# Memory heads as three passes over high and low halves, with the queries split straight from PSUM

## The chip, the cores and the metric

The kernel runs on one core of a Trainium2 chip. The metric is the device time of one execution in microseconds (us), the lower the better. A second figure, the span, is the time between the first and the last instruction that the profiler saw on the core. The engines are named as the profile names them: PE (TensorE, matmuls and transposes), PEld (its weight loads), DVE (VectorE), ACT (ScalarE), POOL (GpSimd) and SP (the queue that issues DMAs).

## The reference, cut to what matters

The program is a stack of several blocks in 32-bit floats over 512 tokens of width 1024. The change touches only the memory heads of its first two layers. Each layer normalises the tokens, projects them, runs twelve main heads (a forgetting attention in layer 0, a retention in layer 1) and four memory heads against 256 memory rows, gates all sixteen heads and projects out.

```python
def mem_cross_attention(q_mem, mem_n, w_kv):
    B, S, _ = q_mem.shape                                   # S = 512
    kv = mem_n @ w_kv
    km, vm = split_cols(kv, [MEM_W, MEM_W])
    q = q_mem.reshape(B, S, N_MEM_HEADS, HEAD_DIM)          # 4 heads of 128
    km = km.reshape(B, -1, N_MEM_HEADS, HEAD_DIM)           # 256 memory rows
    vm = vm.reshape(B, -1, N_MEM_HEADS, HEAD_DIM)
    s = jnp.einsum('bshd,bmhd->bhsm', q, km).astype(jnp.float32) / math.sqrt(HEAD_DIM)
    p = jax.nn.softmax(s, axis=-1).astype(vm.dtype)
    return jnp.einsum('bhsm,bmhd->bshd', p, vm).reshape(B, S, MEM_W)
```

In first_block each layer does `h = rmsnorm(x, norm_g[i])`, `proj = h @ w_in`, the main heads, `memo = mem_cross_attention(q_mem, mem_n, w_mem_kv[i])`, `o = concatenate([main, memo]) * silu(z)` and `x = x + o @ w_out[i]`.

## The kernel before, in words

Every large matmul is done in three passes over halves. A 32-bit operand is split into a high half (a copy to the type fp32r) and a low half (the value less the high half, again fp32r), and PE forms high x high, high x low and low x high. Weights arrive as tiles of 128x1024 in a ring of five raw buffers. For each tile ACT writes the high half (`wh`, `copy` at L2208), and DVE (tiles 0 to 72, L1264) or POOL (nearly all later ones, L2855) writes the low half (`wl`) by a subtraction. Both halves stand in rings of three, so the tile of number u + 2 is split while PE is at tile u.

The order of work on each engine is written out by hand, one function per engine: `tensor`, `vector`, `scalar`, `gpsimd`, `sync`. An object `Feed` walks the same plan on each of them. `feed.take()` moves on by one weight tile and puts the split of the tile two ahead into the engine's queue at that place. Between some of these tiles the plan has tiles of another matrix ("ada"), which DVE multiplies by a column and adds up (L1272, L1233). In layer 0 all of them cost DVE two instructions each. A wait on a semaphore holds the whole queue of its engine.

The rmsnorm of the tokens is put off. PE multiplies the tokens unscaled, and the scale of each token (`R` for layer 0, `RS` for layer 1, as a column `rcol`) is applied when a projection leaves PSUM. The queries of two memory heads come from one unit of PE, `unit_f(("qm", i))`. `store_q` on DVE multiplies them by the scale and by -1/sqrt(128) into `Qt`, in plain 32 bits. For head h of layer l the chain is then:

- `mem_scores`: PE multiplies four blocks of 128 tokens of `Qt` with the keys `km` (256 rows), in plain 32 bits, into banks 2 and 3.
- `mem_begin`: DVE takes the least score of each token (two reductions, L1336), ACT does four exponentials with the sum of each row (L2205). `mem_end`: DVE takes reciprocals of the sums and multiplies (L1346).
- `mem_turn`: PE transposes the probabilities into banks 4 and 7. ACT copies the first to `PT`, DVE the second (L1355).
- `mem_attend`: PE multiplies `PT` with the values `vm` in plain 32 bits into bank 5. DVE applies the gate (`finish`), and ACT and DVE or POOL split the result.

Each step is put into the queues beside a unit of ordinary projection, which is meant to cover the latency of the step before it. In layer 0 the order on PE is: queries of heads 0 and 1 (weight tiles 1, 2), keys (3 to 6), gate of heads 0 and 1 (7, 8), scores 0, values (9 to 12), turn 0, scores 1, keys of layer 1 (13, 14), attend 0, queries of heads 2 and 3 (15, 16), turn 1, scores 2, keys (17, 18), attend 1, values (19, 20), gate of heads 2 and 3 (21, 22), turn 2, scores 3, values (23, 24), attend 2, the first keys of the main heads (25, 26), turn 3, the first queries (27, 28), attend 3. In layer 1 the four heads stand between the units of their own queries and gates (two weight tiles each) in the same manner, attend 2 comes straight behind scores 3, and turn 3 and attend 3 stand in the first pair of retention heads.

`X` holds the tokens. In layer 1 seven of its eight tiles are written to DRAM (`keep_x`) and brought back (`bring_x`), since other buffers lie over them.

## Time and profile before

| | before |
|---|---|
| median of 3 runs | 1593.48 us (1593.42 to 1593.5) |
| the profiled execution | 1593.27 us |
| its span | 1591.5 us |
| PE busy | 1581.3 us, 99% |
| DVE busy | 994.7 us, 62% |
| ACT busy | 761.7 us, 48% |
| POOL busy | 602.9 us, 38% |
| granted clock of PE | 1.0 of full speed all through |

The span lies 1.8 us below the execution's own time. Busy times are averages over the whole span; what an engine has to spare at a given place is read from that place. In a timeline each row has the start, the duration, the engine, the line, the operation, what it writes and reads, the number of instructions merged (x8), and in brackets the idle time before it with what ended it. Neighbouring instructions of one engine overlap: the next one starts a little before the one before it has ended. So the cost of one in a row of many is the distance between starts.

### The profile page before, as it was taken

To read this page: it belongs to the slowest core of one execution; us is meant where nothing else is said; L and a number is where in the kernel's file an instruction comes from. 1 tells how busy PE (TensorE), PEld (TensorE's weight loads), DVE (VectorE), ACT (ScalarE), POOL (GpSimd) and SP (SyncE) were. 2 spreads that over 40 slices of the span, in tenths; PEclk is the share of its full clock that TensorE was granted. 3 is DMA by queue.
4 is the path that set the end of the run, shared out by engine and by line. 5 is a ranking of instruction groups with operands and counts; after the bars stand their busy time and mean duration, and the time that the engine had idled before them with its cause. 6 is when DMAs were issued, how large, how long until landed. Compare 5 with 4: busy or idle time off the path is not lost.

```text
span 1591.5 us, 21843 instructions
## 1 busy us (share of the span) xinstructions
PE 1581.3 (99%) x8856; PEld 1360.8 (86%) x8856; DVE 994.7 (62%) x1477; ACT 761.7 (48%) x1143; POOL 602.9 (38%) x301
## 2 busy tenths in 40 slices
PE   9999999999999999999999999999999999999998
PEld 7888898889888888888888777889888789999997
DVE  7888867676765365455553767782356785555554
ACT  7533443343432334555556465424435645555554
POOL 1002112221245334455556333353223225555552
PEclk9999999999999999999999999999999999999999
DMA  6554434333466423233323331122111232232321
GB/s 245 172 172 147 142 117 144 109 132 126 130 214 212 150 68 119 94 106 106 106 94 137 126 120 66 53 107 83 40 54 67 80 106 107 93 106 93 106 93 54
DMA packets 54413, 182.95 MB, mean 115 GB/s; under 512 B 6556, under 2 KB 7196, under 8 KB 53928
## 3 DMA queue, kind: packets, MB, share of 16 engines
q1 hardware_dynamic: 54312, 181.55, 33.1%
q8 instruction: 70, 1.15, 0.3%
q14 instruction: 31, 0.25, 0.1%
HBM read 174.42 MB, written 3.96 MB: 112 GB/s over the span
## 4 chain that ended last, share of the span: by engine, by line
PE 93%; DVE 4%; ACT 1%; issue 1%; DMA 0%; POOL 0%; SPq 0%; DVEq 0%
PE banks L468 91%; PE banks L471 2%; DVE ACC L1300 0%; DVE TM L1858 0%; DVE wl L1264 0%; DVE X L1233 0%; DVE HL L1233 0%; ACT T L2205 0%; DVE XW L2105 0%; DMA raw<-wst_dram 0%; ACT HH L2205 0%; DVE TM L1868 0%; ACT wh L2208 0%; ACT FHI L2208 0%; DVE ada L1233 0%
## 5 line engine op out<-in xcount | busy, mean ns | idle before, releaser
L2855 POOL TENSOR_TENSOR wl<-raw,wh 128x1024 fp32r<-128x1024 f32 x139 | 346.8, 2498 | 387.7 <-ACT wh L2208 387.7
L468 PE MATMUL banks<-HH,wh 128*128 128x512 f32 (+2 forms) x944 | 362.1, 386 | 1.9 <-ACT HH L2205 1.5
L468 PE MATMUL banks<-HL,wh 128*128 128x512 f32 (+2 forms) x944 | 353.0, 380 | 0.4 <-DVE HL L1233 0.4
L2208 ACT ACTIVATE wh<-raw 128x1024 fp32r<-128x1024 f32 x246 | 257.3, 1051 | 188.6 <-PE banks L468 185.3
L468 PE MATMUL banks<-HH,wl 128*128 128x512 f32 (+1 forms) x936 | 251.4, 380 | 0.6 <-DVE wl L1264 0.5
L468 PEld LDWEIGHTS banks<-HH,wh 128*128 128x128 f32 (+1 forms) x944 | 177.2, 188 | 39.4 <-ACT HH L2205 2.6
L468 PEld LDWEIGHTS banks<-HL,wh 128*128 128x128 f32 (+1 forms) x944 | 176.6, 188 | 35.4 <-DVE HL L1233 1.8
L468 PEld LDWEIGHTS banks<-HH,wl 128*128 128x128 f32 x936 | 172.1, 188 | 35.8 <-issue 1.5
L468 PE MATMUL banks<-wh,HH 128*128 128x256 f32 x448 | 127.8, 285 | 0.0
L468 PE MATMUL banks<-wl,HH 128*128 128x256 f32 x448 | 126.7, 283 | 0.0
L468 PE MATMUL banks<-wh,HL 128*128 128x256 f32 x448 | 126.7, 283 | 0.0
L1264 DVE TENSOR_TENSOR wl<-raw,wh 128x1024 fp32r<-128x1024 f32 x82 | 100.5, 1238 | 24.1 <-ACT wh L2208 24.1
L468 PE MATMUL banks<-OH,wh 128*128 128x512 f32 x256 | 102.9, 402 | 0.0
L468 PE MATMUL banks<-OL,wh 128*128 128x512 f32 x256 | 99.8, 390 | 0.0
L468 PE MATMUL banks<-FLO,wh 128*128 128x512 f32 x256 | 99.8, 390 | 0.0
L468 PE MATMUL banks<-FHI,wh 128*128 128x512 f32 x256 | 99.7, 390 | 0.0
L2868 POOL TENSOR_TENSOR OL<-T,OH 128x512 fp32r<-128x512 f32 x21 | 28.1, 1338 | 179.7 <-ACT OH L2208 179.7
L468 PEld LDWEIGHTS banks<-wh,HL 128*128 128x128 f32 x448 | 85.7, 191 | 0.5 <-issue 0.2
L468 PEld LDWEIGHTS banks<-wh,HH 128*128 128x128 f32 x448 | 85.7, 191 | 0.5 <-issue 0.2
L468 PEld LDWEIGHTS banks<-wl,HH 128*128 128x128 f32 x448 | 85.7, 191 | 0.0
L2860 POOL TENSOR_TENSOR SL<-WS,SH 128x1024 fp32r<-128x1024 f32 x24 | 57.9, 2413 | 46.1 <-ACT SH L2208 46.1
L2893 POOL TENSOR_TENSOR CM<-CB,mask 128x512 f32<-128x512 f32 x12 | 26.9, 2244 | 125.1 <-DMA CB<-sums_dram 89.3
(432 smaller groups left out, 3299.5 us busy)
## 6 DMA issues: line engine op xcount, KB each, us to landing
raw<-wst_dram SPq DMA_DIRECT2D x294, 512.0 KB, 3.3
X<-xT_dram SPq DMA_DIRECT2D x8, 512.0 KB, 6.0
CB<-sums_dram SPq DMA_DIRECT2D x12, 256.0 KB, 3.3
D<-dec_dram SPq DMA_DIRECT2D x12, 256.0 KB, 2.7
out_dram<-XT SPq DMA_DIRECT2D x8, 256.0 KB
x_dram<-X SPq DMA_DIRECT2D x3, 512.0 KB, 6.2
QS<-QX SPq DMA_DIRECT2D x24, 64.0 KB, 2.6
KSw<-KX SPq DMA_DIRECT2D x24, 64.0 KB, 2.0
```

The lines of the kernel that those rows point to most:

```text
L468: return pe.eng.matmul(dst, w, x, start=start, stop=stop, skip_group_check=True)
L471: return pe.eng.transpose(dst, x, ident[:, :])
L1264: tt(wl[:, q, :], raw[:, i % NRAW, :], wh[:, q, :].bitcast(F32), ALU.subtract).then_inc(*by_dve("low", u))
L2208: return eng.activation(dst, src, ACT.Copy)
L2855: tt(wl[:, q, :], raw[:, i % NRAW, :], wh[:, q, :].bitcast(F32), ALU.subtract).then_inc(*by_pool("low", u))
L2860: tt(SL_[:, v % NS, :], WS[:, v % 2, :], SH_[:, v % NS, :].bitcast(F32), ALU.subtract).then_inc(*by_pool("sums low", u))
L2868: tt(OL[:, tile, :], t[:, :], OH[:, tile, :].bitcast(F32), ALU.subtract).then_inc(*by_pool("l", "o", l, tile))
L2893: tt(CM[:, :].rearrange("p (i m) -> p i m", i=4), CB[:, :].rearrange("p (i m) -> p i m", i=4), mask[:, :].rearrange("p (i m) -> p i m", i= ...
```

## The change

The memory heads of both layers get the same treatment as the large matmuls. The queries are split from PSUM without the token scale, ACT writing the high half and DVE the low half. ACT and POOL split keys and values once per layer. ACT copies both transposed blocks of probabilities as high halves, and DVE subtracts for both low halves. The scale of the tokens moves into the softmax: the scores are unscaled, the maximum is taken and multiplied by the column of scales, and each exponential takes the scale as a column. One attend of layer 1 moves behind a weight tile, and `X` is now kept in DRAM whole. New high and low buffers lie over `X` (`QH`, `KMH`, `VMH`, `MPL`), over `km` and `vm` themselves (`KML`, `VML`), and over `PT` (`MPH`).

```diff
+    KMH, KML = at("KMH", [128, 4, 256], 48, F32R), [at("KML%d" % l, [128, 4, 256], (108, 156)[l], F32R) for l in range(2)]
+    VMH, VML = at("VMH", [128, 2, T], 52, F32R), [at("VML%d" % l, [128, 2, T], (112, 160)[l], F32R) for l in range(2)]
+    MPH, MPL = at("MPH", [128, 1024], C0 + 21, F32R), at("MPL", [128, 1024], 56, F32R)
...
         def mem_scores(l, h):                                   # tensor
-            pe.wait_ge(done("q", ("qm", 2 * l + h // 2), h % 2), done("kept", ("km", l, h // 2), 0))
+            pe.wait_ge(done("mq high", l, h), done("mk low", l, h // 2))
             for i in range(4):
-                b = 2 + i // 2
-                pe.wait_ge(*free[b])
-                mm(bank[b][:, 256 * (i % 2):256 * (i % 2) + 256], Qt[:, h % 2, 128 * i:128 * i + 128], km[l][:, h, :],
-                   i % 2 == 0, i % 2 == 1).then_inc(*by_pe("m scored", l, h, i))
+                o = bank[2 + i // 2][:, 256 * (i % 2):256 * (i % 2) + 256]
+                pe.wait_ge(*free[2 + i // 2])
+                mm(o, QH[:, h % 2, 128 * i:128 * i + 128], KMH[:, h, :], i % 2 == 0, False)
+                mm(o, QH[:, h % 2, 128 * i:128 * i + 128], KML[l][:, h, :], False, False)
+            pe.wait_ge(done("mq low", l, h))
+            for i in range(4):
+                o = bank[2 + i // 2][:, 256 * (i % 2):256 * (i % 2) + 256]
+                mm(o, QL[:, h % 2, 128 * i:128 * i + 128], KMH[:, h, :], False, i % 2 == 1).then_inc(*by_pe("m scored", l, h, i))
...
         def mem_attend(l, h):                                   # tensor
-            pe.wait_ge(done("kept", ("vm", l, h // 2), 0), *free[5])
+            c = slice(128 * h, 128 * h + 128)
+            pe.wait_ge(done("mv low", l), *free[5])
+            for j in range(2):
+                pe.wait_ge(done("m ph", l, h, j))
+                mm(bank[5], VMH[:, j, c], MPH[:, T * j:T * j + T], j == 0, False)
+                mm(bank[5], VML[l][:, j, c], MPH[:, T * j:T * j + T], False, False)
             for j in range(2):
                 pe.wait_ge(done("m pt", l, h, j))
-                e = mm(bank[5], vm[l][:, j, 128 * h:128 * h + 128], PT[:, T * j:T * j + T], j == 0, j == 1)
+                e = mm(bank[5], VMH[:, j, c], MPL[:, T * j:T * j + T], False, j == 1)
...
         mem_scores(1, 3)
-        mem_attend(1, 2)                                        # also in vector and scalar
...
-            unit_f(("rqk", p), beside=(lambda: ret_sum(2 * p - 2)) if p else None)
+            unit_f(("rqk", p), beside=(lambda: ret_sum(2 * p - 2)) if p else lambda: mem_attend(1, 2))
...
+        def query_low(l, h):                                    # vector, in place of store_q
+            j = h % 2
+            dve.wait_ge(done("mq high", l, h))
+            stt(QL[:, j, :], bank[j], QSCALE, QH[:, j, :].bitcast(F32), ALU.mult, ALU.subtract).then_inc(*by_dve("mq low", l, h))
+            by_dve.also("kept", ("qm", 2 * l + h // 2), j)
...
         def mem_begin(l, h):                                    # vector
-            for i in (1, 3):
-                dve.wait_ge(done("m scored", l, h, i))
-                dve.wait_ge(now["nmx free"])
-                eng.tensor_reduce(nmx[:, i - 1:i + 1], bank[2 + i // 2].rearrange("p (i m) -> p i m", i=2), AX.X,
-                                  ALU.min).then_inc(*by_dve("m least", l, h))
+            for i in (0, 2):
+                dve.wait_ge(done("m scored", l, h, i + 1), now["nmx free"], done("scale col", ("x0", "x1")[l]))
+                eng.tensor_reduce(nmx[:, i:i + 2], bank[2 + i // 2].rearrange("p (i m) -> p i m", i=2), AX.X,
+                                  ALU.max).then_inc(*by_dve())
+            dve.wait_ge(by_dve.last())
+            stt(nmx[:, 0:4], nmx[:, 0:4], -1.0, rcol[:, 2:6], ALU.mult, ALU.mult).then_inc(*by_dve("m least", l, h))
...
         def mem_turn(l, h):                                     # vector
-            dve.wait_ge(done("m turned", l, h, 1), now["pt read"])
-            eng.tensor_copy(PT[:, T:2 * T], bank[7]).then_inc(*by_dve("m pt", l, h, 1))
+            for j in range(2):
+                dve.wait_ge(done("m ph", l, h, j), done("x kept", 3) if l else done("square", "x0", 7), now["pt read"])
+                tt(MPL[:, T * j:T * j + T], bank[(4, 7)[j]], MPH[:, T * j:T * j + T].bitcast(F32),
+                   ALU.subtract).then_inc(*by_dve("m pt", l, h, j))
...
+        def query_high(l, h, *marks):                           # scalar
+            j = h % 2
+            act.wait_ge(done("unit", ("qm", 2 * l + h // 2), j), done("m scored", l, h - 2, 3) if h > 1 else None, *marks)
+            fn(QH[:, j, :], bank[j], ACT.Copy, scale=QSCALE).then_inc(*by_act("mq high", l, h))
+
+        def keys_high(l, j, *marks):
+            act.wait_ge(done("kept", ("km", l, j), 0), *marks)
+            copy(KMH[:, 2 * j:2 * j + 2, :], km[l][:, 2 * j:2 * j + 2, :]).then_inc(*by_act("mk high", l, j))
+
+        def values_of_memory_high(l, *marks):
+            act.wait_ge(done("kept", ("vm", l, 1), 0), *marks)
+            copy(VMH[:, :, :], vm[l][:, :, :]).then_inc(*by_act("mv high", l))
...
-                   scale=-1.0, accum_out=sm[:, i:i + 1]).then_inc(*by_act("m exp", l, h, i))
+                   scale=rcol[:, 2 + i:3 + i], accum_out=sm[:, i:i + 1]).then_inc(*by_act("m exp", l, h, i))
...
         def mem_turn(l, h):                                     # scalar
-            act.wait_ge(done("m turned", l, h, 0), now["pt read"])
-            copy(PT[:, 0:T], bank[4]).then_inc(*by_act("m pt", l, h, 0))
+            for j in range(2):
+                act.wait_ge(done("m turned", l, h, j), now["pt read"])
+                copy(MPH[:, T * j:T * j + T], bank[(4, 7)[j]]).then_inc(*by_act("m ph", l, h, j))
...
         scales("x0", T, R[:, :], 2)                             # scalar
+        for h in range(2):
+            query_high(0, h, done("l", "x0", 7), done("square", "x0", 7))
         feed.unit()
...
         feed.unit()
+        for j in range(2):
+            keys_high(0, j)
         act.wait_ge(m, done("eps"))
         fn(CB[:, :], CB[:, :], ACT.Ln, bias=one).then_inc(*by_act("gate log"))
...
         mem_values(0, 1, 6)
+        values_of_memory_high(0)
         mem_turn(0, 0)
         mem_begin(0, 1)
         feed.unit()
         mem_attend(0, 0)
         feed.unit()
+        for h in range(2, 4):
+            query_high(0, h)
...
         project_out(0, {(0, 0): [lambda: fox_turn(11)], (0, 1): [lambda: fox_attend(11)]})
+        for j in range(2):
+            keys_high(1, j, done("x kept", 1), done("l", "x1", 3))
+        values_of_memory_high(1, done("x kept", 2), done("l", "x1", 5))
         feed.unit(lambda: scales("x1", T, RS[:, :], 2, done("unit", ("out", 0, 3), 1)))
+        for h in range(2):
+            query_high(1, h)
...
+        def keys_low(l, j):                                     # gpsimd
+            c = slice(2 * j, 2 * j + 2)
+            pool.wait_ge(done("mk high", l, j), done("kept", ("km", l, j), 0))
+            tt(KML[l][:, c, :], km[l][:, c, :], KMH[:, c, :].bitcast(F32), ALU.subtract).then_inc(*by_pool("mk low", l, j))
+
+        def values_of_memory_low(l):
+            pool.wait_ge(done("mv high", l), done("kept", ("vm", l, 1), 0))
+            tt(VML[l][:, :, :], vm[l][:, :, :], VMH[:, :, :].bitcast(F32), ALU.subtract).then_inc(*by_pool("mv low", l))
...
         def keep_x(i):                                          # sync
-            n = 2 if i < 3 else 1
-            sp.wait_ge(done("kept", ("out", 0, i), n - 1))
-            dma(kept_x[:, 2 * i:2 * i + n, :], X[:, 2 * i:2 * i + n, :]).then_inc(*x_out[i]("x kept", i))
+            sp.wait_ge(done("kept", ("out", 0, i), 1))
+            dma(kept_x[:, 2 * i:2 * i + 2, :], X[:, 2 * i:2 * i + 2, :]).then_inc(*x_out[i]("x kept", i))
```

## Rows read from the trace of the kernel before

**Rows 1.** The page: PE's busy line, and DVE's busy tenths in 40 slices.

```profile
PE 1581.3 (99%) x8856; PEld 1360.8 (86%) x8856; DVE 994.7 (62%) x1477; ACT 761.7 (48%) x1143; POOL 602.9 (38%) x301
...
DVE  7888867676765365455553767782356785555554
```

**Rows 2.** Timeline of PE: columns start us, duration us, engine, line, operation.

```profile
149.65 0.36 PE L468 MATMUL banks<-wh,HH 128*128 128x256 f32 x1
149.85 0.28 PE L468 MATMUL banks<-wh,HL 128*128 128x256 f32 x1
149.97 0.28 PE L468 MATMUL banks<-wl,HH 128*128 128x256 f32 x1
...
553.27 1.07 PE L468 MATMUL banks<-HH,wl 128*128 128x512 f32 x4
554.18 1.89 PE L468 MATMUL banks<-km,Qt 128*128 128x256 f32 x8
...
620.18 1.88 PE L468 MATMUL banks<-PT,vm 128*128 128x512 f32 x4
...
622.01 0.28 PE L468 MATMUL banks<-wh,HL 128*128 128x256 f32 x1
```

**Rows 3.** Timeline of DVE in layer 0.

```profile
49.47 0.69 DVE L1233 SCALAR_TENSOR_TENSOR Zt<-T,Zt 128x512 f32<-128x512 f32 x1 [1.73 <-ACT T L2205]
...
62.94 2.35 DVE L1264 TENSOR_TENSOR wl<-raw,wh 128x1024 fp32r<-128x1024 f32 x2
...
69.09 0.18 DVE L1343 RECIPROCAL rs<-sum 128x4 f32<-128x4 f32 x1 [2.00 <-ACT Sc L2205]
...
72.75 2.35 DVE L1264 TENSOR_TENSOR wl<-raw,wh 128x1024 fp32r<-128x1024 f32 x2
...
84.00 0.69 DVE L1233 SCALAR_TENSOR_TENSOR Qt<-banks,R 128x512 f32<-128x512 f32 x1
84.61 1.22 DVE L1264 TENSOR_TENSOR wl<-raw,wh 128x1024 fp32r<-128x1024 f32 x1
```

**Rows 4.** Timeline of PE in layer 0, where it takes up a newly split tile.

```profile
62.81 1.03 PE L471 MATMUL banks<-ident,Sc 128*128 128x128 f32 x8
...
74.73 1.07 PE L468 MATMUL banks<-HH,wl 128*128 128x512 f32 x4
...
94.65 0.35 PE L468 MATMUL banks<-wh,MH 128*128 128x256 f32 x1 [0.61 <-DVE wl L1264]
...
123.74 1.19 PE L468 MATMUL banks<-HH,wl 128*128 128x512 f32 x4
```

**Rows 5.** Timeline of ACT, in layer 0 and at the start of layer 1.

```profile
45.47 1.28 ACT L2205 ACT_TABLE_LOAD   x1
...
48.80 0.63 ACT L2205 ACTIVATE T<-Zt 128x512 f32<-128x512 f32 x1
...
84.44 0.60 ACT L2208 ACTIVATE PT<-banks 128x512 f32<-128x512 f32 x1 [4.76 <-PE banks L471]
...
541.81 0.72 ACT L2205 ACTIVATE HH<-X,par 128x512 fp32r<-128x512 f32 x1 [1.99 <-DVE X L1541]
...
548.01 0.69 ACT L2205 ACTIVATE RS<-banks,eps 128x512 f32<-128x512 f32 x1 [2.19 <-PE banks L468]
```

**Rows 6.** Timelines of POOL and DVE where both read SBUF at once.

```profile
77.06 1.61 POOL L2868 TENSOR_TENSOR OL<-T,OH 128x512 fp32r<-128x512 f32 x1 [41.22 <-ACT OH L2208]
...
77.42 2.33 DVE L1233 SCALAR_TENSOR_TENSOR ada<-raw,scc,ada 128x1024 f32<-128x1024 f32 x1
...
615.81 2.40 POOL L2855 TENSOR_TENSOR wl<-raw,wh 128x1024 fp32r<-128x1024 f32 x1 [2.71 <-ACT wh L2208]
615.83 2.93 DVE L1600 TENSOR_TENSOR T<-QX,COS 128x512 f32<-128x512 f32 x1
```

**Rows 7.** Timelines of SP (last tokens brought back) and of DVE (their use).

```profile
896.74 0.43 SPq L3072 DMA_DIRECT2D X<-x_dram  x1
...
919.17 0.68 DVE L1541 TENSOR_TENSOR X<-X,banks 128x512 f32<-128x512 f32 x1
```

More of the change, by code:

```diff
@@ L1519, in vector @@
                     feed.take()
-                dve.wait_ge(done("v high", p, 2 * (t // 2) + 1), done("f out", 2 * p - 1) if p else None)
+                dve.wait_ge(done("v high", p, 2 * (t // 2) + 1), done("f out", 2 * p - 1) if p else done("m out", 0, 3))
                 stt(VL[:, t, :], bank[t // 2][:, 256 * (t % 2):256 * (t % 2) + 256], rcol[:, 2 + t:3 + t],
@@ L1588, in vector @@
         mem_scores(1, 3)
-        mem_attend(1, 2)
         def keep_k(p):
@@ L1661, in vector @@
         for p in range(6):
-            feed.unit((lambda: ret_norm(2 * p - 2)) if p else None)
+            feed.unit((lambda: ret_norm(2 * p - 2)) if p else lambda: mem_attend(1, 2))
             if p:
@@ L2267, in tanh_bank @@
             fn(t[:, :], bank[b], ACT.Tanh, scale=0.5).then_inc(*by_act("tanh", tag, j))
+        def query_high(l, h, *marks):
[8 more added lines that the diff above has]
+            copy(VMH[:, :, :], vm[l][:, :, :]).then_inc(*by_act("mv high", l))
         def mem_begin(l, h):
-            act.wait_ge(done("m least", l, h), now["s read"], now["sm free"])
+            act.wait_ge(done("m least", l, h), done("scale col", ("x0", "x1")[l]), now["s read"], now["sm free"])
             for i in range(4):
                 fn(S4[:, i, :], bank[2 + i // 2][:, 256 * (i % 2):256 * (i % 2) + 256], ACT.Exp, bias=nmx[:, i:i + 1],
-                   scale=-1.0, accum_out=sm[:, i:i + 1]).then_inc(*by_act("m exp", l, h, i))
+                   scale=rcol[:, 2 + i:3 + i], accum_out=sm[:, i:i + 1]).then_inc(*by_act("m exp", l, h, i))
             now["sm free"] = done("m recip", l, h)
         def mem_turn(l, h):
-            act.wait_ge(done("m turned", l, h, 0), now["pt read"])
-            copy(PT[:, 0:T], bank[4]).then_inc(*by_act("m pt", l, h, 0))
+            for j in range(2):
+                act.wait_ge(done("m turned", l, h, j), now["pt read"])
+                copy(MPH[:, T * j:T * j + T], bank[(4, 7)[j]]).then_inc(*by_act("m ph", l, h, j))
             now["s read"] = done("m turned", l, h, 1)
@@ L2370, in scalar @@
             for j in range(2):
-                act.wait_ge(done("kept", ("fk", p), j))
+                act.wait_ge(done("kept", ("fk", p), j), None if p else done("m scored", 0, 3, 3))
                 copy(KH[:, j, :], Kt[:, j, :]).then_inc(*by_act("k high", p, j))
@@ L2429, in scalar @@
         feed.unit(lambda: mem_attend(1, 0))
+        for h in range(2, 4):
+            query_high(1, h)
         mem_turn(1, 1)
@@ L2486, in scalar @@
         for p in range(6):
-            feed.unit((lambda: even_norm(p - 1)) if p else None)
+            feed.unit((lambda: even_norm(p - 1)) if p else lambda: mem_attend(1, 2))
             if p:
@@ L2883, in gpsimd @@
         units(6)
+        def keys_low(l, j):
[5 more added lines that the diff above has]
+            tt(VML[l][:, :, :], vm[l][:, :, :], VMH[:, :, :].bitcast(F32), ALU.subtract).then_inc(*by_pool("mv low", l))
+        for j in range(2):
+            keys_low(0, j)
+        values_of_memory_low(0)
         finish(0, 12)
@@ L2915, in gpsimd @@
                 finish(0, 11)
-        units(2)
+        for j in range(2):
+            keys_low(1, j)
+        feed.unit()
+        values_of_memory_low(1)
+        feed.unit()
         feed.unit(lambda: finish(1, 12))
         feed.unit(lambda: finish(1, 13))
-        finish(1, 14)
         def weighted_low(h):
@@ L2924, in gpsimd @@
         for p in range(6):
-            feed.unit((lambda: finish(1, 2 * p - 2)) if p else None)
+            feed.unit(lambda: finish(1, 2 * p - 2 if p else 14))
             feed.unit()
@@ L3064, in keep_x @@
         def keep_x(i):
-            n = 2 if i < 3 else 1
-            sp.wait_ge(done("kept", ("out", 0, i), n - 1))
-            dma(kept_x[:, 2 * i:2 * i + n, :], X[:, 2 * i:2 * i + n, :]).then_inc(*x_out[i]("x kept", i))
+            sp.wait_ge(done("kept", ("out", 0, i), 1))
+            dma(kept_x[:, 2 * i:2 * i + 2, :], X[:, 2 * i:2 * i + 2, :]).then_inc(*x_out[i]("x kept", i))
         def bring_x(i):
-            n = 2 if i < 3 else 1
             sp.wait_ge(done("x kept", i))
-            dma(X[:, 2 * i:2 * i + n, :], kept_x[:, 2 * i:2 * i + n, :]).then_inc(*x_in[i]("x back", i))
+            dma(X[:, 2 * i:2 * i + 2, :], kept_x[:, 2 * i:2 * i + 2, :]).then_inc(*x_in[i]("x back", i))
         for n in range(16):
```

9 lines of the change are left out of this document (4 added, 5 removed).

## The prediction

> **What bounds the kernel now.** I read the page's busy line first: PE is busy in 99% of the span [rows 1]. So the time is PE's own work plus its few waits, and a change pays by what it takes off PE and costs by what it adds to PE's waits. Then I read PE's rows around the memory heads for prices [rows 2]. Last I read the engines that feed PE there. DVE's slices of 39.8 us are at 8 tenths from the second to the fourth, where layer 0's heads lie, and at 3 to 6 tenths from the fourteenth to the sixteenth (517 to 637 us), where layer 1's lie [rows 1]. Layer 0 is thus the place where added work on DVE can reach PE. It already does: PE waits 0.61 us for a low half at 94.65, and the four matmuls at 123.74 take 1.19 instead of 1.07 us, a wait of 0.12 us [rows 4].
>
> **What PE saves.** The prices are distances between starts [rows 2].
>
> - Four passes of 512 columns take 554.18 - 553.27 = 0.91 us, 0.227 each. One of 256 columns takes 149.97 - 149.85 = 0.12.
> - Scores before: eight records, (1.89 - 0.38)/7 = 0.216 each with 0.38 for a single one, together 1.73. After: twelve passes of 256 columns, 12 x 0.12 = 1.44. Saved: 0.29.
> - Attend before: from 620.18 to the next unit's first matmul, 622.01 - 0.12 = 621.89, so 1.71. After: six passes of 512 columns, 1.36. Saved: 0.35.
> - The first three-pass matmul behind transposes costs 0.20 instead of 0.12 (149.65 to 149.85). Six of the eight scores stand behind a turn, so 6 x 0.08 = 0.5 is lost. The plain matmul that stood there may pay as much already; that bound is 0.
>
> Eight heads give 8 x 0.29 + 8 x 0.35 = 5.1, less 0.5: **4.6 us saved** (4.6 to 5.1).
>
> **What DVE and ACT get in layer 0.** All of it stands in front of splits that PE waits for.
>
> - *keys_high*: two ACT copies of 128x512, 0.63 each, 0.54 from start to start, 1.1 together. They stand before the table load at 45.47, from which ACT works without a pause to the tanh at 48.80, and DVE waits 1.73 for that tanh [rows 3, 5]. So the whole 1.1 passes on to DVE.
> - *Second reading of the maximum* (128x4): about 0.2 per head, by the 0.18 of the reciprocal of the same size [rows 3]; bounds 0.1 and 0.3.
> - *Exponentials with a scale column*: no row has one beside a bias column. A column in place of a constant takes a 128x512 copy from 0.63 to 0.72 [rows 5]. That is 0.09 each, 0.36 for the four in a row for which DVE waits (2.00 now) [rows 3]. The other bound is 0.
> - *Second subtraction in mem_turn*: 0.60, as 84.00 to 84.61 [rows 3].
> - *Queries*: before, DVE took them from PSUM itself at 84.00. Now ACT's copy (0.60, as at 84.44) [rows 5] comes first: 0.6.
>
> Instructions that only change their kind (a greatest for a least, a query's low half for a stored query) keep shape, engine and place and cost what they did.
>
> **Where it reaches PE: three places.**
>
> *Tile 15 (head 0 and 1 in front).* DVE makes the split at 72.75, done at 73.9, and PE uses it at 74.73 [rows 3, 4]: 0.8 spare. Delays of DVE: 1.1 + 0.2 + 0.36 before head 1's splits at 62.94, then 0.6 + 0.2 + 0.36, together 2.8. PE comes earlier by two scores and one attend, 0.85. Without more: 2.8 + 0.85 - 0.8 = 2.85.
>
> To this comes POOL. Its subtraction for the values (128x1024, 2.40 us as at 615.81) follows ACT's copy of them. PE ends the values at 62.81 (the transposes start there) [rows 4]; two ACT moves of 256 columns and a copy of 1024, by the 0.63 us per 512 columns about 2 us, come next, so POOL asks at about 64.8. DVE is then in the first of the two splits that started at 62.94 (now 64.5 to 65.7), and the second is next. The rows show what follows: where both engines read SBUF, DVE's 0.69 us instruction at 615.83 took 2.93, 2.24 longer, and the one at 77.42 took 2.33 while POOL had asked at 77.06, before it [rows 6]. I take 2.2, with 0 if they miss each other. Tile 15 then costs 2.85 + 2.2 = **5.1 us**.
>
> The Trainium skill (SBUF — State Buffer, "SBUF: two separate sides") says the same as a rule: the port pair that VectorE and GpSimd share is an exclusive lock, held for a whole instruction, and it concerns VectorE only with two SBUF inputs or in a two-port mode. By that rule the split would wait the full 2.4, which would make the sum 0.2 higher; the new subtractions read PSUM and would not be held.
>
> *Tile 19 (head 2 in front).* No slack: PE waits 0.61 already [rows 4]. Added on DVE: query 0.6, subtraction 0.6, small 0.2, exponentials 0.36, together 1.8; PE is earlier by 0.29 + 0.35 - 0.08 = 0.56. Added wait: **2.35 us**.
>
> *Tile 25 (head 3 in front).* No slack either (0.12 waited). Added: 0.6 + 0.2 + 0.36 = 1.15 and 0.56: **1.7 us**. Head 3's own chain stands before a whole unit of projections with no wait now and gets no more than 1.2 later: nothing.
>
> Sum of added waits 5.1 + 2.35 + 1.7 = 9.15.
>
> **Layer 1** I cost at nothing, and this is the cover. ACT gets keys and values, 2.2 us, before the normalisation; it is idle 2.19 before 548.01 beyond its table load of 1.28, which the trace shows started early, so the start moves by about 0.1 [rows 5]. POOL's three subtractions (2.4 us, and twice half of it) fall where it makes one split of 2.4 us [rows 6] per tile of 24 x 0.227 = 5.4 us on PE. The queries no longer wait for the token scale, and DVE has half its time free [rows 1]. Without that cover each head would cost what it does in layer 0, 1 to 2 us. The moved attend goes behind one weight tile on PE, DVE, ACT and POOL; the new passes wait for two subtractions instead of one copy, and this tile (5.4 us) hides them. It issues no DMA. On SP the last kept pair of tiles is 512 KB instead of 256. It goes out right behind the sum of the last tile, and its first overwriter stands behind two units of PE, 21 us. Brought back at 896.74, it is read at 919.17 [rows 7]. Both have ten us and more to land, and the weight loads queued behind them are five tiles ahead of their use.
>
> **The sum.** 1593.27 (the profiled execution) - 4.6 + 9.15 = 1597.8. It stands 0.2 below the median, so against that 1593.48 + 4.5 = **1598.0 us**.
>
> **Rivals.**
>
> - *POOL and DVE miss each other.* POOL's request must fall into DVE's first split, 64.5 to 65.7, and mine is at 64.8. If DVE's delay there is below about 0.9 instead of 1.66, or if DVE goes first, the 2.2 falls away: 1595.8.
> - *The splits have the cover, faster.* PE gets its 4.6 and the delays are absorbed: 1588.9. For it speaks that DVE's ada products need not be done at that place and that DVE has pauses at every head. Against it: these pauses are DVE's waits for ACT's exponentials [rows 3], which get longer, and tiles 19 and 25 have no slack [rows 4]. It decides if the added delay of each chain is under 0.5 us, so that the waits grow by less than 1.4 in all.
> - *Layer 1 stalls too.* ACT holds 2.2 us of copies in front of the split and the scales of layer 1, and two of them wait for DMAs of `X` to DRAM. If PE waits for that once and for one head's chain: 1598.0 + 2.5 = 1600.5.
> - *The extremes of the unknown prices.* With exponentials that cost the same, tile 15 gets 0.7 and tiles 19 and 25 0.36 each less: 1596.6.
>
> **Chances and range.** The forecast case has 0.60, the miss 0.20, the cover 0.10, layer 1's stall 0.10. Within 0.2% is 3.2 us, which is about what a measurement of this kernel can tell from no change: 1590.3 to 1596.7. Slower: 0.55 of the first case and all of the last but a little, 0.63. Same: nearly all of the second and the edge of the first, 0.28. Faster: 0.09. The range takes in the miss with the cheap exponentials (1595.8 - 1.4 = 1594.4) and reaches at the top to layer 1's stall: 1594.0 to 1600.4. It leaves the cover out.
>
> **What would show it.** The eight scores would stand at 1.44 us from start to next start and attends at 1.36. PE's waits for DVE's low halves would be near 5, 3 and 1.8 us at tiles 15, 19 and 25, in a list of waits that now has 1.1 in all. One DVE split near 66 us would last about 3.4 instead of 1.22. PE's busy time would fall by some 4 to 5 us while the span grows. The prediction is wrong if the waits of PE between 40 and 130 us come to less than 5 us in total, or if the exponentials keep their 2.00.

## The result, and the profile after

The changed kernel takes 1601.19 us in the median (1599.68 to 1602.33, 4 runs) against 1593.49 us (1593.42 to 1593.68, 4 runs): ratio 1.0047, 95% interval 1.0035 to 1.0059. It is slower, by 7.7 us where 4.5 were forecast, and outside the range. The profiled execution took 1601.36 us with a span of 1599.6 us.

The page of the changed kernel, its first lines (busy time by engine; then DVE's busy tenths in 40 slices), to set beside [rows 1]:

```profile
span 1599.6 us, 21981 instructions
...
PE 1580.5 (99%) x8904; PEld 1364.2 (85%) x8904; DVE 1002.4 (63%) x1493; ACT 776.3 (49%) x1165; POOL 613.7 (38%) x307
...
DVE  7788867666766366444554667782256795555554
```

PE is busy 0.8 us less and the span is 8.1 us longer, so PE stands still for 8.9 us more. The list of PE's waits says where:

```profile
PE banks L473 <- DVE wl L1277: 7.2, 6, 3.0
PE banks L473 <- DVE PT L1655: 2.9, 4, 1.0
```

The columns are the total, the number of waits and the longest. The first line was 1.1 us before. The second is new and has nothing to do with the memory heads: `PT` at L1655 are the weighted scores of the retention heads.

To see where the time goes, follow the lateness of PE: the start of one instruction here less the start of the same one before. PE's timeline of the changed kernel at the places of [rows 4] and [rows 2], and four places behind them:

```profile
57.93 0.36 PE L473 MATMUL banks<-wh,MH 128*128 128x256 f32 x1 [0.58 <-DVE wl L1277]
...
77.52 1.21 PE L473 MATMUL banks<-HH,wl 128*128 128x512 f32 x4 [1.85 <-DVE wl L1277]
...
99.41 0.36 PE L473 MATMUL banks<-wh,MH 128*128 128x256 f32 x1 [3.02 <-DVE wl L1277]
...
103.89 0.37 PE L473 MATMUL banks<-wh,ML 128*128 128x256 f32 x1
...
131.14 1.19 PE L473 MATMUL banks<-HH,wl 128*128 128x512 f32 x4 [1.12 <-DVE wl L1277]
...
547.93 0.39 PE L473 MATMUL banks<-HH,wh 128*128 128x512 f32 x1
...
626.35 0.28 PE L473 MATMUL banks<-wh,HL 128*128 128x256 f32 x1
...
850.53 0.39 PE L473 MATMUL banks<-RPH,VH 128*128 128x512 f32 x1
...
1590.43 0.95 PE L473 MATMUL banks<-ones,T 128*128 128x1 f32 x8
```

| place | before | after | lateness |
|---|---|---|---|
| tile 11 | 57.05 | 57.93 | 0.88 |
| tile 15 | 74.73 | 77.52 | 2.79 |
| tile 19, its first matmul | 94.65 | 99.41 | 4.76 |
| tile 19, behind slow matmuls | 97.71 | 103.89 | 6.18 |
| tile 25 | 123.74 | 131.14 | 7.40 |
| layer 1 begins | 540.89 | 547.93 | 7.04 |
| layer 1's last attend is over | 622.01 | 626.35 | 4.34 |
| retention heads are over | 842.38 | 850.53 | 8.15 |
| last sums | 1582.34 | 1590.43 | 8.09 |

So there are four parts: layer 0 loses 7.0 us (0.4 of it at the start of the kernel, before any changed instruction), 1.42 of them in one stretch of slow matmuls; layer 1's heads win 2.70; the retention heads, in which no instruction of PE behind that last attend is changed, lose 3.81; the rest is level. These are parts of one profiled execution, whose 1601.36 us lie close to the median.

The slow stretch is seen in the windows of PE (columns: window, busy us with the number of instructions, granted clock, DMA share, GB/s):

```profile
95.00:100.00 5.00, 1.98 (x12) 1.00 0.17 42
100.00:102.00 2.00, 2.00 (x15) 0.66 0.89 258
102.00:104.00 2.00, 2.00 (x11) 0.50 0.92 344
104.00:106.00 2.00, 2.00 (x19) 0.98 0.23 88
```

Right behind the wait of 3.02 us the granted clock falls to 0.50, the lower of its two levels (1.2 GHz), and from 100.9 us fifteen matmuls of 256 columns start 0.21 us apart instead of 0.12. That is the 1.42 us between 99.41 and 103.89.

DVE's timeline in layer 0, to set beside [rows 3], and POOL's:

```profile
65.27 2.36 DVE L1277 TENSOR_TENSOR wl<-raw,wh 128x1024 fp32r<-128x1024 f32 x2
67.54 1.29 DVE L1376 TENSOR_TENSOR MPL<-banks,MPH 128x512 fp32r<-128x512 f32 x2
68.74 1.28 DVE L1354 TENSOR_REDUCE nmx<-banks 128x2 f32<-128x512 f32 x2
70.06 0.16 DVE L1246 SCALAR_TENSOR_TENSOR nmx<-nmx,tq 128x4 f32<-128x4 f32 x1
72.59 0.18 DVE L1363 RECIPROCAL rs<-sum 128x4 f32<-128x4 f32 x1 [2.37 <-ACT Sc L2226]
...
95.65 1.28 DVE L1246 SCALAR_TENSOR_TENSOR ada<-raw,sc,ada 128x1024 f32<-128x1024 f32 x1
96.84 1.28 DVE L1246 SCALAR_TENSOR_TENSOR ada<-raw,scc,ada 128x1024 f32<-128x1024 f32 x1
98.04 2.36 DVE L1277 TENSOR_TENSOR wl<-raw,wh 128x1024 fp32r<-128x1024 f32 x2
```

```profile
65.97 3.92 POOL L2940 TENSOR_TENSOR VML<-vm,VMH 128x1024 fp32r<-128x1024 f32 x1 [16.11 <-ACT VMH L2229]
```

The unknown prices came out at the values taken: four exponentials with a scale column keep DVE waiting 2.37 us instead of 2.00 (0.37; 0.36 forecast), the 128x4 step costs 0.16 (0.2), the second subtraction 0.60. POOL asks at 65.97, while DVE is in the first of two splits, as forecast; but here DVE's second split goes ahead undelayed (two in 2.36) and POOL is the one that is held (3.92 instead of 2.40).

In the retention heads the same pair of instructions shows it, in DVE's timeline. Before:

```profile
702.20 0.69 DVE L1603 TENSOR_TENSOR QS<-QS,SIN 128x512 f32<-128x512 f32 x1 [3.19 <-DMA QS<-QX]
```

and in the changed kernel:

```profile
709.08 0.69 DVE L1624 TENSOR_TENSOR QS<-QS,SIN 128x512 f32<-128x512 f32 x1 [5.02 <-DMA QS<-QX]
```

The DMAs that swap the halves of a rotated query land 1.8 us later, though the last of them is issued 4.5 us behind the end of ACT's `QX` in both kernels. PE's timeline shows the end of that chain, four times:

```profile
674.78 0.38 PE L473 MATMUL banks<-RQH,RKH 64*128 64x256 f32 x1 [0.53 <-DVE PT L1655]
716.40 0.38 PE L473 MATMUL banks<-RQH,RKH 64*128 64x256 f32 x1 [1.02 <-DVE PT L1655]
757.97 0.38 PE L473 MATMUL banks<-RQH,RKH 64*128 64x256 f32 x1 [1.02 <-DVE PT L1655]
798.68 0.39 PE L473 MATMUL banks<-RQH,RKH 64*128 64x256 f32 x1 [0.32 <-DVE PT L1655]
```

A pair of heads takes 40.3 us before, and 41.6 where PE waits 1.02: the loss is a little more than the wait that is shown. The chain has about 0.7 us to spare: a swap that is 1.2 us late costs a wait of 0.53, one that is 1.8 late costs 1.02.

### The profile page after: what moved, and what is told of

It is laid out like the page before. It is cut to its first block, busy times and chain, and to the rows that moved or that the text cites. A ratio compares the mean times of both kernels' runs of the same rounds, so it can differ in the third digit from the quotient of the medians.

```text
span 1599.6 us, 21981 instructions
## 1 busy us (share of the span) xinstructions
PE 1580.5 (99%) x8904; PEld 1364.2 (85%) x8904; DVE 1002.4 (63%) x1493; ACT 776.3 (49%) x1165; POOL 613.7 (38%) x307
## 3 DMA queue, kind: packets, MB, share of 16 engines
q8 instruction: 70, 1.15, 0.3%
## 4 chain that ended last, share of the span: by engine, by line
PE 85%; DVE 7%; ACT 3%; issue 1%; DMA 1%; POOL 1%; SPq 1%; DVEq 0%; ACTq 0%
PE banks L473 83%; PE banks L476 2%; DVE wl L1277 1%; DMA QS<-QX 1%; DVE ACC L1313 1%; ACT wh L2229 1%; ACT Sc L2226 0%; DMA maskf<-cst_dram 0%; DVE TM L1879 0%; POOL wl L2903 0%; ACT T L2226 0%; ACT L2226 0%; DVE ada L1246 0%; DVE X L1246 0%; DVE HL L1246 0%
```

## The experiments

### The two layers apart

layer1_only keeps the change in layer 1 and takes it back in layer 0; layer0_only is the other way round (with the moved attend and the larger piece of `X` taken back too). The edit in both is a choice by layer in each helper:

```diff
+NEW = (1,)          # layer0_only: (0,)
...
+        def mem_scores(l, h):
+            (mem_scores_halves if l in NEW else mem_scores_plain)(l, h)
```

> Layer 0's four heads are as in the kernel before; layer 1's four heads, its moved attend and the whole X to DRAM are as in the changed kernel. The prediction costed layer 1 at PE's saving alone: 4 x (0.29 + 0.35) less 3 x 0.08 = 2.3 us. If that holds and the new waits of the retention pairs (2.9 us for PT in the changed kernel) come from layer 0's lateness or from chance, the time is 1593.5 - 2.3 = 1591.2 us, ratio 0.9986, with no wait of PE for PT over 0.1 us between 640 and 800 us. Rival: the waits of the retention pairs belong to layer 1's change. Then they are here too, and the time is 1591.2 + 2.9 = 1594.1 us, ratio 1.0004.

> Layer 0's four heads are as in the changed kernel, layer 1 is as in the kernel before. Waits of PE between 40 and 130 us come to about 7 us (near 0.6, 1.9, 3.0 and 1.1) and the granted clock falls for about 4 us behind the 3 us wait at 99 us, as in the changed kernel. If the waits of the retention pairs come from layer 0's lateness, the time is the changed kernel's plus layer 1's 2.3 us of PE: 1601.2 + 2.3 = 1603.5 us, ratio 1.0063. Rival, they belong to layer 1's change: 1603.5 - 2.9 = 1600.6 us, ratio 1.0045, and no wait for PT there.

layer1_only: 1593.19 us (1591.62 to 1594.89, 10 runs), ratio 0.9998 (0.9988 to 1.0007). layer0_only: 1605.92 us, ratio 1.0079 (1.0064 to 1.0094). Neither theory fits by itself. Both kernels have the waits for `PT`, 2.7 us in four places and 2.3 us in three, and in the retention heads their PE falls back by 3.85 and 3.14 us. So it is neither layer 1's change nor the lateness of layer 0: layer1_only comes to these heads 2.1 us early and loses as much. By PE's starts layer 1's heads win 2.70 us in layer1_only as well. The profiled execution of layer1_only is the slowest of its ten (1594.89, 1.7 us over the median), so its 3.85 us are the upper end of what the runs of this kernel show and not their middle.

layer0_only is 2.4 us above the expectation, and its timeline of DVE and POOL says why:

```profile
64.99 4.55 DVE L1305 TENSOR_TENSOR wl<-raw,wh 128x1024 fp32r<-128x1024 f32 x2
```

```profile
65.69 2.78 POOL L3000 TENSOR_TENSOR VML<-vm,VMH 128x1024 fp32r<-128x1024 f32 x1 [16.12 <-ACT VMH L2277]
```

The same two instructions in the same order as in the changed kernel, but now POOL goes first and DVE's second split takes 3.42 us instead of 1.22 (3.4 was forecast) and is 2.2 late. PE pays it at tile 14, where it waits for ACT's high half, whose queue stands behind the exponentials of head 1:

```profile
75.47 0.50 PE L476 MATMUL banks<-HH,wh 128*128 128x512 f32 x1 [2.31 <-ACT wh L2277]
...
79.44 0.73 PE L476 MATMUL banks<-HH,wl 128*128 128x512 f32 x2 [1.86 <-DVE wl L1305]
```

Five profiles of this case have these instructions in this order: layer0_only, fill_wait_19 and pool_splits show it so, the changed kernel and after_fetch_moved the other way. Below, this choice between POOL and DVE is called the toss.

### Does the wait at tile 19 bring the clock down?

```diff
         mem_attend(0, 1)
+        pe.wait_ge(*free[7])
+        for n in range(12):
+            mm(bank[7], HH[:, 0, 0:128], HH[:, 1, :], True, True)
         mem_values(1, 0, 7)
```

> The changed kernel, and on PE twelve more matmuls of 512 columns (12 x 0.227 = 2.7 us) between attend 1 and tile 19, in the place where PE waits 3.02 us at 99.41. Their result is overwritten. Theory: PE's clock falls because of the idle stretch there, and the slow passes behind it cost about 2 us. Then the granted clock stays at 1.0 between 100 and 106 us, the wait at tile 19 shrinks to about 0.3, and the time is about 2 us under the changed kernel's: near 1599.2 us, ratio 1.0036. Rival: the fall has another cause (it comes with the waits as such or at random): the granted clock falls all the same and the time stays at 1601 us or goes up to 1603 where the matmuls are not hidden.

1602.18 us (1598.79 to 1603.4, 4 runs), ratio 1.0051 (1.0036 to 1.0066), where 1599.2 was expected. The windows of PE:

```profile
95.00:100.00 5.00, 5.00 (x33) 1.00 0.06 24
100.00:102.00 2.00, 1.71 (x9) 1.00 0.26 47
102.00:104.00 2.00, 2.00 (x18) 1.00 0.85 266
104.00:106.00 2.00, 2.00 (x19) 1.00 0.94 328
```

The clock stays at 1.00 and the wait falls to 0.29: the idle stretch was the cause. The median doesn't show the gain. POOL went first in this profile, which costs 2.3 us at tile 14 that the changed kernel's profile has not; in how many of the runs it did is not known. Beside layer0_only, where POOL went first too, PE's lateness at tile 25 is 8.39 instead of 9.25 us, and the kernel began 0.6 us later: about 1.5 us gained, for the 1.42 read from the slow stretch.

### POOL makes three of the splits

```diff
-DVE_LOW = frozenset([*range(73), 164, *range(186, 194)])
+BY_POOL = (15, 19, 25)
+DVE_LOW = frozenset([*(u for u in range(73) if u not in BY_POOL), 164, *range(186, 194)])
```

(and POOL takes tile 15's behind its subtraction of the values)

> The changed kernel with the low halves of weight tiles 15, 19 and 25 made by POOL instead of DVE (2.4 us each in place of 1.2). Theory that the queue of DVE is what is late: at tiles 15, 19 and 25 PE then waits less; each is one split (1.2 us) less on DVE's chain, and tiles 16, 20 and 26 are the next in question. If nothing is lost to the two engines' use of SBUF, waits fall by 1.2 at each tile and the clock keeps up at 19: 1601.2 - 3.5 - 2 = 1595.7 us, ratio 1.0014. Rival, by the row in which DVE's instruction at 80.91 lasts 2.32 instead of 1.27 beside POOL: each split on POOL holds DVE for 1.2 to 2.4 us in instructions that read SBUF, so nothing is won and up to 1.2 us per tile lost: 1601 to 1604 us.

1599.47 us (1598.03 to 1601.09, 4 runs), ratio 1.0038 (1.0023 to 1.0053), where 1595.7 was expected: about 1.7 us under the changed kernel, with intervals that overlap. Between the theories. PE's waits for DVE's halves fell from 7.2 to 2.3 us, but 2.2 for POOL's half, 2.3 for ACT's (with a granted clock of 0.50 between 76 and 78 us behind it) and 0.4 for a query's low half came in their place; one scaling of the probabilities beside POOL's split took 3.31 us for four instead of 1.14.

### What makes the swap DMAs late?

Both layers' halves of the change have one thing in common: PE gets more instructions (8904 matmuls for 8856). The view of the DMA queues counts packets by queue. Besides the kernel's own queue q1 there is q8, of kind "instruction", with 70 packets and 1.15 MB in each kernel, one of 16 KB about every 21 us here. Going through the stretch in windows of 1 us gives the time of each. In the changed kernel the window from 706 to 707 us, in which swaps are under way, has one:

```profile
q1 hardware_dynamic: 122, 0.17, 53.9%
q8 instruction: 1, 0.02, 6.4%
issues: line engine op xcount, KB each, median us to landing
KSw<-KX SPq DMA_DIRECT2D x2, 64.0 KB, 3.3
```

6.4% of 16 engines for 1 us is one of the 16 DMA engines for all of it. My reading, which no trace shows directly, is that a swap is done only when the last engine has done its part. Before, the packet of this pair comes at 705 to 706 us, when `QS` had been used since 702.20. So the suspicion is that the packets are PE's instructions, and that the count of them ahead sets where a fetch falls. The traces bear this out: number the packets of q8 from 0, and in all fourteen profiles packet k of the retention stage comes when PE has started 256 k + 152 to 256 k + 208 instructions (matmuls and weight loads), however many the kernel has. The kernel has a knob for that which costs next to nothing: 18 matmuls of zeros with which PE passes the time until its first data.

```diff
-        for n in range(18):
-            mm(bank[7], Z0[:, 0:128], Z0[:, :], True, True)
+        for n in range(40):
+            mm(bank[7][:, 0:230], Z0[:, 0:128], Z0[:, 0:230], True, True)
```

before_fetch_moved is the kernel before with this edit alone. layer1_only_fetch_moved has 68 matmuls of 136 columns, after_fetch_moved 55 of 168, and after_fetch_moved_values_later adds one line that keeps POOL back until DVE's second split is done, and so settles the toss:

```diff
             keys_low(0, j)
+        pool.wait_ge(done("low", 14))
         values_of_memory_low(0)
```

> The kernel before; only its 18 warm-up matmuls of 512 columns, which PE does while it waits for its first data, are now 40 of 230 columns: the same columns, 22 matmuls (44 instructions of PE with their weight loads) more. Theory: the 3 to 4 us that the retention pairs cost in the changed kernel and in both halves of the change are instruction fetches (packets of 16 KB on the queue q8, about 21 us apart) that fall into the swap DMAs QS and KSw; in the kernel before they fall 5 to 8 us behind the start of a swap, and the count of PE's instructions ahead sets where. 44 instructions move them some 3.5 us earlier, into the swaps: PE then waits for DVE's PT three or four times and the time grows by 2.5 to 4 us, to about 1596.5 us, ratio 1.0019. Rival: the pairs' waits come from the lateness or the DMAs of the change, or are noise: nothing changes, ratio 1.000, no wait for PT.

> layer1_only with 68 warm-up matmuls of 136 columns in place of 18 of 512: 100 instructions of PE more, which by the theory move the fetches 8 us earlier, out of the swaps (from 2.5 to 8 us behind the start of a swap to between 5.5 before it and its start). Then PE's waits for PT (2.7 us in layer1_only) are gone and the retention pairs cost what they cost in the kernel before: 1593.5 - 2.7 (layer 1's saving as the starts of PE's matmuls show it in layer1_only) = 1590.8 us, ratio 0.9983. Rival, the waits belong to layer 1's change: as layer1_only, 1593.2 us, ratio 0.9998.

> The changed kernel with 55 warm-up matmuls of 168 columns in place of 18 of 512: 74 instructions of PE more, fetches 6 us earlier, from 1 before to 4 behind the start of a swap to 7 to 2 before it. By the fetch theory the PT waits (2.9 us, 3.8 us with what does not show as a wait) are gone: 1601.2 - 3.5 = 1597.7 us, ratio 1.0027. Rival: 1601 us as before.

> As after_fetch_moved, and POOL starts its subtraction for the memory values of layer 0 only when DVE's second split (tile 14) is done. Theory: who gets the SBUF side that DVE and POOL share is a toss between DVE's queued second split and POOL's waiting instruction. In the changed kernel's profile DVE's went first (two splits in 2.36 us, POOL's took 3.92), in three others POOL's did (4.55 us, PE's wait at 75.5 us 2.3 longer). With the wait the two splits always take 2.36 and POOL's 2.4, the extra wait of 2.2 us never comes, and the runs' spread (2.65 us in the changed kernel) shrinks: 2.2 us under those runs in which POOL goes first, so about 1.5 us under after_fetch_moved in the median, 1596.2 us, ratio 1.0018. Rival: the toss is no matter and the time is that of after_fetch_moved.

| kernel | median (lowest to highest) | ratio (95% interval) | waits for `PT` in the profile |
|---|---|---|---|
| before_fetch_moved | 1595.10 (1594.93 to 1595.86) | 1.0009 (1.0000 to 1.0018) | 1.4 us, 2 times |
| layer1_only_fetch_moved | 1592.93 (1592.28 to 1593.53) | 0.9995 (0.9986 to 1.0004) | 1.7 us, 3 times |
| after_fetch_moved | 1601.89 (1599.10 to 1603.09) | 1.0049 (1.0035 to 1.0063) | 1.3 us, 2 times |
| after_fetch_moved_values_later | 1598.93 (1598.53 to 1600.80) | 1.0037 (1.0024 to 1.0050) | 1.1 us, 2 times |

The kernel before gets the waits from nothing but 22 more warm-up matmuls:

```profile
670.54 0.39 PE L468 MATMUL banks<-RQH,RKH 64*128 64x256 f32 x1 [0.49 <-DVE PT L1634]
711.89 0.38 PE L468 MATMUL banks<-RQH,RKH 64*128 64x256 f32 x1 [0.92 <-DVE PT L1634]
```

and it gets them in the two pairs into whose swaps the fetches now fall. With the time at which ACT has `QX` ready as zero, its fetches stand at 5.5, 7.1, 8.8 and 10.6 us in the second to fifth pairs, and the waits are in the second and third (the first pair's fetch stands at 6.0 and no wait is shown there). The fastest of its ten runs (1594.93) is slower than all but one (1595.30) of the 22 of the kernel before that ran beside them. The expectation was too high in size (1.5 us for 2.5 to 4), since the fetches drift by 1.6 to 1.8 us a pair and only two were hit. The same drift explains why the other three lost only part of their waits: a shift that clears the first pairs brings the fetches into the last. Over the ten profiles up to here, with six pairs each, `QS` is used 6.3 to 7.4 us behind `QX` where no fetch of q8 falls between 2 and 6.5 us behind it; where one does, 7.8 to 8.7 us, but for two at 2.3 and 2.5 (7.3 and 7.1). PE waits for `PT` in 28 of the 31 pairs in which a fetch falls between 2.1 and 8.5 us behind `QX`, and in none of the 29 others.

By PE's starts from 622 to 842 us of the kernel before, the retention heads lose 1.8, 2.3, 1.7 and 1.5 us in the four kernels of the table. The medians follow less well. layer1_only_fetch_moved stands at 1592.93 where 1590.8 was expected. after_fetch_moved stands at 1601.89 where 1597.7 was expected, no lower than the changed kernel, and its profiled execution (1599.10) is the fastest of its four: that its median gained from the moved fetches is not shown. after_fetch_moved_values_later stands at 1598.93 for 1596.2.

The toss's share can't be read from these four: the medians of the last two kernels lie 3 us apart, but their runs overlap (1599.1 to 1603.1, 1598.5 to 1600.8), and in both profiles DVE went first. Nor did the spread shrink as expected: 2.27 us over five runs with the toss settled, 2.65 over four in the changed kernel, and 3.27 over ten in layer1_only, which has no such subtraction in layer 0.

### All pairs cleared, and the queue of DVE relieved

From here a shift was worked out that clears all pairs: 176 instructions more, so that the next fetch of the row stands 9 us and more behind `QX` (106 warm-up matmuls of 64 columns). And a theory on layer 0 was left: ahead of the splits of tiles 15, 19 and 25 DVE has 2.4 us of ada products in its queue that nobody waits for (95.65 and 96.84 in the timeline above).

```diff
+        late = []
+
         def split(i, u):
+            split_now(i, u)
+            while late:
+                ada_now(*late.pop(0))
...
         def ada(i, g, k):
+            if 9 <= feed.made <= 30:
+                late.append((i, g, k))
+            else:
+                ada_now(i, g, k)
```

> layer1_only with 106 warm-up matmuls of 64 columns in place of 18 of 512: 176 instructions of PE more, fetches some 14 us earlier, so that the next one of the row stands 9 to 20 us behind QX in every pair, clear of the swaps (the traces so far show waits where a fetch stands 2 to 8 us behind QX and none elsewhere). No wait for PT, each pair 40.3 us; 1593.6 - 2.7 = 1590.9 us, ratio 0.9983. Rival, the pairs' waits belong to layer 1's change as well: at 1592.9 or above, ratio 0.9995 or more.

> The changed kernel; on DVE, for the weight tiles 9 to 30, the ada products that stand ahead of a split in its queue are put behind that split. Theory: the waits at tiles 15, 19 and 25 are DVE's queue coming late, and 2.4 us of ada products stand right ahead of the splits. Then the waits 1.85, 3.02 and 1.12 fall to about 0, 0.6 and 0, the clock does not fall behind 99 us (1.4 us), and where POOL's instruction goes first (2.2) part is still hidden: some 6 to 7 us less, 1594.7 us, ratio 1.0007. Rival: the deferred products hold the raw buffers longer, the next loads come late and ACT's high halves with them: PE's waits for DVE's halves go over into waits for ACT's, and the time stays over 1598 us.

> The kernel before with the same edit (ada products behind the split, tiles 9 to 30). Its waits for DVE's halves in layer 0 are 0.61 and 0.12 us, so 0.7 us at most is to be had: 1592.9 us, ratio 0.9995. Rival: loads come late, up to 1 us more: 1594.6, ratio 1.0006.

> The changed kernel with ada products behind the splits (tiles 9 to 30), POOL's subtraction for layer 0's values held until DVE's split of tile 14 is done, and 78 warm-up matmuls of 96 columns (120 instructions more, fetches 9.7 us earlier, out of the swaps but for the last pair). By the three theories: 1601.2 - 6.5 (ada and the clock) - 1 (the toss, what is left of 2.2) - 3 (fetches) = 1590.7 us, ratio 0.9982. Rival, each of them is only partly right or they overlap: 1593 to 1596 us.

| kernel | median (lowest to highest) | ratio (95% interval) |
|---|---|---|
| layer1_only_fetch_clear | 1591.83 (1591.44 to 1592.07) | 0.9989 (0.9980 to 0.9997) |
| after_ada_behind_split | 1598.65 (1598.24 to 1599.01) | 1.0032 (1.0020 to 1.0044) |
| before_ada_behind_split | 1593.24 (1592.69 to 1594.65) | 0.9997 (0.9988 to 1.0007) |
| after_all_mended | 1594.13 (1593.63 to 1596.48) | 1.0005 (0.9996 to 1.0014) |

*layer1_only_fetch_clear* has no wait for `PT` left in its list of PE's waits, here whole:

```profile
PE banks L476 <- ACT HH L2272: 1.9, 2, 1.0
PE banks L476 <- DVE wl L1304: 1.3, 3, 0.6
PE banks L476 <- DVE Z L1449: 1.2, 1, 1.2
PE banks L476 <- DVE HL L1273: 0.6, 2, 0.4
PE banks L476 <- DVE X L1609: 0.3, 1, 0.3
```

Its pairs take 40.3 us each: PE comes to the retention heads 1.42 us early and leaves them 1.42 early. It is the one version whose interval lies wholly under the kernel before, by 1.9 us in the median (2.7 expected); its slowest run (1592.07) is faster than the fastest of the kernel before (1593.17). The missing 0.8 may well be at the front: the first wait above (ACT `HH`) was 1.5 and PE's matmul of tile 19 starts at 95.94 instead of 94.65, so the kernel begins 1.3 us later in this profile, whether by the 106 small matmuls or by chance was not tried.

*after_ada_behind_split* wins 2.5 us of the 6 to 7 expected. The theory of the queue holds at the places it named: 1.85, 3.02 and 1.12 become none, 1.39 and none, and the clock keeps up behind tile 19. But POOL's subtraction (65.17) now holds an ada product of DVE (65.22, 3.43 us instead of 1.28), and what was taken off DVE's front comes back one step on:

```profile
69.84 0.39 PE L473 MATMUL banks<-MH,wl 128*128 128x256 f32 x1 [0.58 <-DVE wl L1284]
75.71 0.50 PE L473 MATMUL banks<-HH,wh 128*128 128x512 f32 x1 [2.31 <-ACT wh L2242]
90.68 0.74 PE L473 MATMUL banks<-KMH,QL 128*128 128x256 f32 x4 [0.34 <-DVE QL L1246]
99.95 0.36 PE L473 MATMUL banks<-wh,MH 128*128 128x256 f32 x1 [1.39 <-DVE wl L1284]
103.48 0.36 PE L473 MATMUL banks<-wh,MH 128*128 128x256 f32 x1 [0.42 <-DVE wl L1284]
```

A chain of head 1 that is late by DVE's 2.2 us reaches PE through ACT, and this order of DVE's work did not mend that. And behind that wait of 2.31 us the clock falls now, as the windows of PE show:

```profile
74.00:76.00 2.00, 0.29 (x1) 1.00 0.14 55
76.00:78.00 2.00, 2.00 (x6) 0.56 0.00 0
78.00:80.00 2.00, 2.00 (x7) 0.59 0.00 0
```

*before_ada_behind_split* came out as expected: its profile has no wait for a weight's low half in layer 0, and its time (1593.24 for 1592.9) is that of the kernel before.

In *after_all_mended* DVE is not held by POOL and the wait for ACT is 0.98, but a query's low half, now behind deferred products, costs 1.82. Its retention heads lose nothing (PE comes to them 1.17 us late and leaves them 1.20 late), so the 3.81 us go away in the changed kernel as well. The three cures together bring 7.1 of the 7.7 us back and no more (1594.13 where 1590.7 was expected): level with the kernel before, where layer 1's gain alone would be 2.7.

## Why the prediction was wrong

**What held.** Slower was right, and by the mechanism named: DVE's queue in layer 0 is late at tiles 15, 19 and 25. The added waits were put at 9.15 us. The changed kernel's profile has 0.58, 0.18, 1.85, 3.02, 0.27 and 1.12 between 40 and 135 us, together 7.0 where [rows 4] had 0.7; layer0_only, in which POOL goes first, has 0.58, 2.31, 1.86, 3.01, 0.27 and 1.11, together 9.1. Prices of PE: scores 1.43 us from start to next start (50.00 to the next weight tile at 51.43). Head by head PE wins 0.25 to 0.3 us on scores and 0.35 on attend: 2.70 in layer 1, where 2.3 were forecast, since the plain matmuls behind transposes paid the 0.08 as well (the bound of 0 that was kept and not taken). The heads of layer 1 do have their cover. One sign that was foreseen did not come: PE's busy time fell by 0.8 us and not by 4 to 5. The slow stretch puts 1.4 us on it; where the rest is was not traced.

**The toss.** The term of 2.2 us for POOL and DVE was right in size and place and is there in three of five profiles. The forecast took it as settled once POOL's request falls into DVE's first split. It does (65.97), but then either may go next. Whether it is a source of the spread of 2.65 us over the changed kernel's runs is not shown, since kernels without it spread as widely (layer1_only by 3.27, and the kernel before by 2.11 over the 22 runs beside before_fetch_moved).

**The step that failed: "Layer 1 I cost at nothing".** The cover named there holds for the heads, but the text stopped at their end. Ahead of the retention heads the change puts 48 matmuls more into PE's queue, and that moves PE's instruction fetches against the swap DMAs, whose chain (swap, rotation, scores, `PT`, PE) has less than 1 us to spare. In the kernel before the fetches happened to stand 8.4 us and more behind `QX`, and 1.1 in the last pair: the worst of it is a key swap of the first pair that lands at 11.1 instead of 9.4 us, and PE doesn't wait for it. With the change they hit four pairs. 3.81 us of the 8.1 are this. before_fetch_moved shows that it needs no part of the change, layer1_only_fetch_clear that it goes away by count alone.

**Two smaller terms were missing.** PE's clock: behind a wait of 3.02 us it was granted at 0.50 for some 3 us, 1.42 us more, and the same wait filled with matmuls (fill_wait_19) did not. And a wait costs more than it shows: the lateness grows by 2.15 us over tile 15's wait of 1.85 and by 1.29 over tile 25's 1.12. At tile 15 part of it is that the matmul that restarts takes 0.34 to its follower instead of 0.23. Over the stage some 1.1 us are left when the other terms are taken off; that is a remainder and not a measurement.

Put together: 0.4 (start) + 6.3 (waits less those of before) + 1.1 + 1.4 - 2.2 = 7.0 in layer 0, then -2.7 and +3.8, which is 8.1. The forecast had 9.15 - 4.6 = 4.5. Layer 0 by itself was forecast at 9.15 - 2.3 = 6.85 and came out at 7.0, and that is luck: the toss fell the other way in this profile (2.2 less than forecast), 1.0 us of waits stood at places that the forecast doesn't name (0.58 at tile 11, 0.18 and 0.27 for ACT), and the clock, the dearer restarts and the start made up the rest. With the fetches where they were before, the changed kernel would stand at about 1601.2 - 3.8 = 1597.4 us, inside the range; this is an estimate. after_fetch_moved_values_later, with the toss settled and 1.5 us of the fetches left, measured 1598.93, which fits it.

## What to carry to other kernels

Count instructions as well as time: where a chain that ends at the busiest engine runs through small DMAs with under a microsecond to spare, the phase of the instruction fetches decides, every added instruction ahead moves it, and a change far away can be blamed for it. Look for the fetch packets in the queues' view, and move them with warm-up instructions, before judging a change of under 0.5%. Where an engine feeds the bound with no slack, as DVE does in layer 0, a change that saves PE 0.65 us per head and costs that engine 1.2 to 1.8 loses; the same change pays where the engine has half its time free, so judge it stage by stage and keep the half that pays.

## What the runs showed of the hardware

- One instruction fetch of 16 KB keeps one DMA engine busy for about 1 us (mostly 5.5 to 8% of 16 engines in windows of 1 us) and makes the last of four swaps of 64 KB land 1 to 1.8 us later. The Trainium skill (Advanced Engine Details and Errata, "ISA Cache") gives a cache line of 16 KB, 256 instructions. The runs agree: 1.15 MB in 70 packets is 16 KB each, and PE's count at packet k is 256 k + 152 to 208 throughout the retention stage of all fourteen profiles. The other queue of this kind, q14 (31 packets of 8 KB), doesn't bring the waits: in the fourth pair it has one 2.6 us behind `QX` both in the changed kernel, where PE waits 1.02 us, and in after_fetch_moved and after_all_mended, where it doesn't wait.
- With POOL waiting and DVE having the next instruction queued, either can get the SBUF side that they share: two splits took 2.36 us in two profiles and 4.55 in three, with POOL's request 0.7 us behind the start of the first in all of them. What decides it stays open.
- PE's granted clock fell to 0.50 behind the wait of 3.0 us at tile 19 in each of the four profiles that have it, and not behind 1.86 us. Around the wait of about 2.3 us at tile 14 it fell in pool_splits and after_ada_behind_split (0.50 and 0.56 between 76 and 78 us; in pool_splits from 75.4 us, 0.3 before the wait ended) and stayed at 1.00 in layer0_only and fill_wait_19. What tells these apart was not tried.
